# Gains applied while a normed activation is split in two, and a new order of the first loads, in a fp32 transformer kernel

## The chip, the cores and the metric

The kernel runs on one core of one Trainium2 chip. The metric is the time of one execution on the device in microseconds (us). The core has five engines with programs of their own that meet only in semaphores: TensorE (PE in the profile) multiplies matrices, VectorE (DVE) and ScalarE (ACT) work on 128 rows at a time, GpSimd (POOL) does so too, and SyncE (SP) issues loads. Loads are carried out by DMA queues; each engine that issues loads has a queue.

## The reference

The input x has 256 tokens of 1024 features, fp32. Two layers run over it, each of three residual steps: a gated feed-forward, a mixer (windowed attention and a short convolution), a gated feed-forward. A norm, a second block of one layer with two kinds of attention, and a last product follow.

```python
def rms_norm(x, gain):
    inv = lax.rsqrt(jnp.mean(x * x, axis=-1, keepdims=True) + NORM_EPS)
    return (x * inv) * gain
for l in range(DEPTH):
    x = x + 0.5 * swiglu(rms_norm(x, ffn1_norm[l]), wg, wu, wd)      # 1024 -> 2816 -> 1024
    z = rms_norm(x, mix_norm[l]) @ w_in[l]                           # attention, convolution
    x = x + mixed @ w_out[l]
    x = x + 0.5 * swiglu(rms_norm(x, ffn2_norm[l]), wg, wu, wd)
x = rms_norm(x, final_norm)
```

## The kernel before

Everything lies transposed: features on the 128 partitions, tokens in the columns. x is kept as eight tiles of 128 features by 256 tokens (`x_res`, KT = 8).

**Split products.** fp32 accuracy comes from three products of reduced-precision parts. A weight tile w (128 x 1024, 512 KB) is loaded into one of four slots of `w_raw`; ScalarE rounds it to `w_hi` (L408), VectorE takes the rest w - w_hi as `w_lo` (L676), and TensorE does hi x hi, lo x hi, hi x lo (L1064 to L1066), 24 products of 256 columns for an output tile of 128 features. SP loads the weights in the order of use; a load waits until the slot's `w_lo` is done. `split_ahead` splits three weight tiles ahead of the one in use.

**The norm.** The root mean square scales columns (tokens) and so may be applied after the product; the gain scales rows and goes in before. For each of the eight tiles k of x:
- ScalarE squares the tile (`square`, L420); GpSimd adds the squares of tiles 0 to 6 up in turn (L345, L348, `acc_step`); TensorE sums over the partitions with a matrix of ones (L1096, and L1098 for the square of tile 7).
- VectorE multiplies by the gain (`scaled`, L689) into a buffer `h_32`, ScalarE rounds that to `h_hi` (`high`, L438), VectorE subtracts to get `h_lo` (`low`, L695).

These stand in four places. At the start, for k = 0 to 7, with the splits of the first three weight tiles between them: the first behind tile 3. In `down` (the last product of each feed-forward), where every second weight tile completes one output tile of x. In `wout` (the mixer's last product), where each weight tile does. In both, VectorE first adds the product to x (L751, L861), then `scaled`, `low`. In `wout` it also splits a weight tile between the two. A norm of its own after the last layer (`norm`, L702, L433) uses `h_32` too and has its gain and root applied at once.

**TensorE behind a norm** (`first_pair`): bank 0 takes the tiles 0 to 6 as their `h_lo` come, then the two sums, then bank 1 takes the tiles 0 to 6, and both take tile 7. Behind the last layer there is no first pair; only the sums stand there, and Ln and Exp on ScalarE wait for them.

**The first loads.** SP issues x in two halves of 512 KB, then the weight tiles. ScalarE issues a small table with all gains. GpSimd issues the loads of constants (2.3 MB, used 200 us later) once the eighth `scaled` is done.

## Time and profile before

| | before |
|---|---|
| median of 3 runs | 1277.93 us (1277.87 to 1278.14) |
| the profiled execution | 1275.89 us, of which the span from the first to the last instruction is 1274.1 |
| TensorE's matmuls, busy | 1239.2 us, 97% of the span |
| VectorE, ScalarE, GpSimd busy | 822.2, 658.6, 147.2 us |
| weight split, ScalarE (L408) and VectorE (L676), mean | 1.1 and 1.3 us |
| small table (57 KB), issued by ScalarE | from 1.24, for 0.40 us |
| chain that ended last | 92% TensorE, 4% VectorE, 2% ScalarE |

The profiled execution is a little shorter than the median. Busy time says what an engine did, not that the others waited for it; what counts is idle time of TensorE and the engine that ends it. Matmuls overlap, so two of them are compared by their starts.

### The profile page before, as it was taken

The page shows a single profiled execution, that of the slowest core. Times are in us where ns is not written, and L with a number is a line of the kernel's source. Part 1 is how long each engine was busy: PE and PEld are TensorE (multiplying, and loading weights), DVE is VectorE, ACT ScalarE, POOL GpSimd, SP SyncE. Part 2 cuts the span into 40 slices and gives each one's busy share as a digit, 9 for nine tenths or more (in the row PEclk, how much of TensorE's full clock was granted, in tenths as well). Part 3 has the DMA queues.
Part 4 walks back from the last instruction along what each step waited for, and adds up shares of the span by engine and source line. Part 5 has one row for each costly group of instructions (what it writes and reads, how often), then busy time and mean ns, then how long its engine had stood idle before and what let it go on. Part 6 is the DMA issues. An engine that isn't in the chain of part 4 may idle for free.

```text
span 1274.1 us, 27430 instructions
## 1 busy us (share of the span) xinstructions
PE 1239.2 (97%) x10074; PEld 1191.6 (94%) x10074; DVE 822.2 (65%) x1378; ACT 658.6 (52%) x1105; POOL 147.2 (12%) x209
## 2 busy tenths in 40 slices
PE   6999999999999999999999999999989989999998
PEld 6999999999999999999999999999978878987888
DVE  6667665867666655667656777667657666535664
ACT  6445543646544545445544555545445656644652
POOL 3000000351000000000001340000021000002540
PEclk9999999999999999999999999999998999999999
DMA  7555654345556644555644346556633320435442
GB/s 285 185 190 186 236 168 144 133 133 199 181 181 207 220 167 151 181 187 202 222 148 165 117 149 198 181 181 224 204 120 121 124 100 22 161 100 174 149 141 83
DMA packets 56197, 210.89 MB, mean 166 GB/s; under 512 B 6672, under 2 KB 8720, under 8 KB 56000
## 3 DMA queue, kind: packets, MB, share of 16 engines
q1 hardware_dynamic: 54048, 203.45, 47.1%
q0 software_dynamic: 1936, 6.47, 1.6%
q8 instruction: 42, 0.69, 0.2%
q14 instruction: 27, 0.22, 0.1%
q10 hardware_dynamic: 144, 0.06, 0.0%
HBM read 208.91 MB, written 1.05 MB: 165 GB/s over the span
## 4 chain that ended last, share of the span: by engine, by line
PE 92%; DVE 4%; ACT 2%; issue 2%; DMA 0%; POOL 0%; DVEq 0%; ACTq 0%; SPq 0%; POOLq 0%
PE bank L1064 27%; PE bank L1066 26%; PE bank L1065 26%; PE bank L1389 2%; DVE w_lo L676 2%; PE bank L1102 1%; PE bank L1372 1%; DVE h_lo L695 1%; PE bank L1359 1%; PE bank L1300 1%; PE bank L1302 1%; PE bank L1301 1%; ACT w_hi L408 1%; PE bank L1354 1%; PE bank L1157 0%
## 5 line engine op out<-in xcount | busy, mean ns | idle before, releaser
L1064 PE MATMUL bank<-h_hi,w_hi 128*128 128x256 f32 (+1 forms) x1992 | 570.3, 286 | 17.3 <-DVE w_lo L676 11.7
L1065 PE MATMUL bank<-h_lo,w_hi 128*128 128x256 f32 (+1 forms) x1992 | 563.0, 283 | 0.0
L1066 PE MATMUL bank<-h_hi,w_lo 128*128 128x256 f32 (+1 forms) x1992 | 562.7, 282 | 0.0
L676 DVE TENSOR_TENSOR w_lo<-w_raw,w_hi 128x1024 fp32r<-128x1024 f32 (+1 forms) x360 | 465.9, 1296 | 81.2 <-ACT w_hi L408 80.5
L408 ACT ACTIVATE w_hi<-w_raw 128x1024 fp32r<-128x1024 f32 (+1 forms) x360 | 397.8, 1109 | 91.8 <-PE bank L1066 68.3
L1064 PEld LDWEIGHTS bank<-h_hi,w_hi 128*128 128x128 f32 x1992 | 378.2, 190 | 27.4 <-issue 22.9
L1066 PEld LDWEIGHTS bank<-h_hi,w_lo 128*128 128x128 f32 x1992 | 379.0, 190 | 0.0
L1065 PEld LDWEIGHTS bank<-h_lo,w_hi 128*128 128x128 f32 x1992 | 376.5, 189 | 0.9
L1064 PE MATMUL bank<-g_hi,w_hi 128*128 128x256 f32 x832 | 230.4, 277 | 0.8 <-DVE x_res L861 0.8
L1065 PE MATMUL bank<-g_lo,w_hi 128*128 128x256 f32 x832 | 229.8, 276 | 0.0
L1066 PE MATMUL bank<-g_hi,w_lo 128*128 128x256 f32 x832 | 229.8, 276 | 0.0
L1064 PEld LDWEIGHTS bank<-g_hi,w_hi 128*128 128x128 f32 x832 | 156.2, 188 | 1.6 <-issue 0.8
L1065 PEld LDWEIGHTS bank<-g_lo,w_hi 128*128 128x128 f32 x832 | 156.2, 188 | 0.0
L1066 PEld LDWEIGHTS bank<-g_hi,w_lo 128*128 128x128 f32 x832 | 156.2, 188 | 0.0
L460 ACT ACTIVATE g_hi<-gated 128x256 f32 (+1 forms) x88 | 37.0, 420 | 167.5 <-DVE gated L731 167.5
L727 DVE TENSOR_TENSOR gated<-bank,rstd 128x256 f32<-128x256 f32 x88 | 37.4, 424 | 97.7 <-PE bank L1066 97.4
L420 ACT ACTIVATE squares<-x_res 128x256 f32<-128x256 f32 (+2 forms) x64 | 26.7, 419 | 120.5 <-DVE x_res L751 97.3
L345 POOL COPY ln_mean<-squares 128x256 f32<-128x256 f32 (+1 forms) x8 | 5.3, 667 | 558.9 <-ACT squares L420 558.9
L456 ACT ACTIVATE silu_gate<-squares 128x256 f32<-128x256 f32 x88 | 37.0, 420 | 59.4 <-DVE squares L723 59.4
L723 DVE TENSOR_TENSOR squares<-bank,rstd 128x256 f32<-128x256 f32 x88 | 37.4, 424 | 46.7 <-PE bank L1066 46.7
L348 POOL TENSOR_TENSOR ln_mean<-ln_mean,squares 128x256 f32<-128x256 f32 (+1 forms) x45 | 44.3, 984 | 183.5 <-ACT squares L420 183.0
L1064 PE MATMUL bank<-y_hi,w_hi 128*128 128x256 f32 (+1 forms) x168 | 50.1, 298 | 0.0
(153 smaller groups left out, 1189.3 us busy)
## 6 DMA issues: line engine op xcount, KB each, us to landing
w_raw<-in_w SPq DMA_DIRECT2D x296, 512.0 KB, 3.3
w_raw<-in_wd SPq DMA_DIRECT2D x64, 704.0 KB, 4.1
rel_bias<-in_relbias POOLq DMA_DIRECT2D x32, 128.0 KB, 2.4
btab_sb<-in_btab POOLq DMA_DIRECT2D x1, 1536.0 KB, 9.6
x_res<-in_xT SPq DMA_DIRECT2D x2, 512.0 KB, 5.0
out_T<-x_res SPq DMA_DIRECT2D x8, 128.0 KB, 1.7
rope_sb<-in_rope POOLq DMA_DIRECT2D x1, 272.0 KB, 3.5
mats_sb<-in_mats POOLq DMA_DIRECT2D x1, 192.0 KB, 3.9
```

What stands on the lines that cost most here:

```text
L348: pool.tensor_tensor(acc[:, 0:n], acc[:, 0:n], sq[:, k % 2, 0:n], ALU.add)\
L408: act.activation(whi[:, slot, 0:cols], raw[:, slot, 0:cols], ACT.Copy).then_inc(hi_ready[slot], 1)
L420: act.activation(sq[:, p, 0:src.shape[-1]], src, ACT.Square).then_inc(sq_done[p], 1)
L456: act.activation(sg[:, p], sq[:, p, 0:T], ACT.Silu).then_inc(silu_done[p], 1)
L460: act.activation(ghi[:, f, :], g32[:, p], ACT.Copy).then_inc(g_hi[p], 1)
L676: dve.tensor_tensor(wlo[:, slot, 0:cols], raw[:, slot, 0:cols], whi[:, slot, 0:cols].bitcast(F32), ALU.subtract).then_inc(lo_ready[slot], 1)
L723: dve.tensor_tensor(sq[:, p, 0:T], bank[2 * p][:, 0:T], rs[:, 0, 0:T], ALU.mult)\
L727: dve.tensor_tensor(g32[:, p], bank[2 * p + 1][:, 0:T], rs[:, 0, 0:T], ALU.mult)\
L1064: pe.matmul(o, h, xh, start=first, stop=False)
L1065: pe.matmul(o, h, xl, start=False, stop=False)
L1066: return pe.matmul(o, lo, xh, start=False, stop=last)
L1389: mm = pe.matmul(o, w, PT[:, v % 4, n * BLK:(n + 1) * BLK], start=n == 0, stop=n == 2)
```

## The change

Four things change together.
- `scaled` goes; `h_32` stays for `norm` alone. `high` reads x itself with the gain as its per-partition scale (a pointer into the table); `low` is one instruction x * gain - h_hi with three operands. In `down` and `wout`, ScalarE does `high` ahead of `square`.
- At the start x comes in four quarters of 256 KB from ScalarE's queue, behind the small table. SP starts with the first weight tile, and waits for the second quarter of x before the second weight tile.
- At the start VectorE does the squares of the odd tiles. The first weight tile is split behind tile 1 (the other two behind tiles 5 and 7, as before on ScalarE).
- GpSimd's loads of constants wait for the eighth `h_lo`.

```diff
@@ -211,7 +211,7 @@
         hi_ready = [sem(f"hi_ready{s}") for s in range(SLOTS)]
         lo_ready = [sem(f"lo_ready{s}") for s in range(SLOTS)]
         w_used = [sem(f"w_used{s}") for s in range(SLOTS)]
-        x_loaded = [sem(f"x_loaded{p}") for p in range(2)]
+        x_loaded = [sem(f"x_loaded{p}") for p in range(KT // 2)]
         g_loaded = sem("g_loaded")
         c_loaded, b_loaded = sem("c_loaded"), sem("b_loaded")
         const_set, second_set = sem("const_set"), sem("second_set")
@@ -292,9 +292,6 @@
         def _(sp):
             for s in raw_full:
                 sp.sem_inc(s, 16 * PRIME)
-            for p in range(2):
-                half = slice(p * KT // 2, (p + 1) * KT // 2)
-                sp.dma_start(x[:, half, 0:T], xT[:, half]).then_inc(x_loaded[p], 16)
 
             def load(src, cols, slot, count):
 
@@ -311,6 +308,8 @@
 
                 with sp.Fori(0, ph.pieces // SLOTS) as j:
                     for r in range(SLOTS):
+                        if name == "gu1" and r == 1:
+                            sp.wait_ge(x_loaded[1], 16)
                         piece(r, j)
                 for i in range(ph.pieces // SLOTS * SLOTS, ph.pieces):
                     piece(i, 0)
@@ -349,7 +348,7 @@
                             .then_inc(acc_step, 1)
 
             add_squares(0)
-            pool.wait_ge(h32_done, KT)
+            pool.wait_ge(h_lo, KT)
             pool.dma_start(mat[:], mats).then_inc(c_loaded, 16)
             pool.dma_start(rop[:], rope).then_inc(c_loaded, 16)
             pool.dma_start(cmask[:], colmask).then_inc(c_loaded, 16)
@@ -401,6 +400,9 @@
             for s in (*hi_ready, *silu_done, pt_done):
                 act.sem_inc(s, PRIME)
             act.dma_start(sml[:], small).then_inc(g_loaded, 16)
+            for p in range(KT // 2):
+                two = slice(2 * p, 2 * p + 2)
+                act.dma_start(x[:, two, 0:T], xT[:, two]).then_inc(x_loaded[p], 16)
 
             def split(slot, cols, count):
                 act.wait_ge(raw_full[slot], count * 16)
@@ -429,13 +431,13 @@
                 act.wait_ge(sum_done, q + 1)
                 rstd(bank[SUM][:, 0:n], 0, D, n, q + 1)
                 for k in range(KT):
-                    act.wait_ge(h32_done, q * KT + k + 1)
+                    act.wait_ge(h32_done, k + 1)
                     act.activation(hhi[:, k * TM:k * TM + n], h32[:, k % 4, 0:n], ACT.Copy).then_inc(h_hi, 1)
 
-            def high(q, k, slot):
-
-                act.wait_ge(h32_done, q * KT + k + 1)
-                act.activation(hhi[:, bass.ds(k * TM, T)], h32[:, slot, 0:T], ACT.Copy).then_inc(h_hi, 1)
+            def high(q, k):
+
+                act.activation(hhi[:, bass.ds(k * TM, T)], x[:, k, 0:T], ACT.Copy,
+                               scale=sml[:, bass.ds(q * KT + k, 1)]).then_inc(h_hi, 1)
 
             def late_rstd(q):
                 act.wait_ge(sum_done, q + 1)
@@ -475,10 +477,10 @@
                         split_ahead(name, nxt, l, i, j, last)
                         if r % 2:
                             p, o2 = r // 2, j if not last else KT // 2 - 1
+                            act.wait_ge(x_ready[p], q * 4 + o2 + (PRIME - 3))
                             act.wait_ge(acc_step, q * 7 + o2 * 2 + p - 1)
-                            act.wait_ge(x_ready[p], q * 4 + o2 + (PRIME - 3))
+                            high(q, o2 * 2 + p)
                             square(p, x[:, o2 * 2 + p, 0:T])
-                            high(q, o2 * 2 + p, p)
 
                 with act.Fori(0, DN // SLOTS - 1) as j:
                     lap(j, False)
@@ -538,20 +540,22 @@
                         act.wait_ge(sum_done, q)
                     else:
                         act.wait_ge(acc_step, q * 7 + o - 1)
+                    high(q, o)
                     square(o % 2, x[:, o, 0:T])
-                    high(q, o, o % 2)
                     if o == KT - 1:
                         split_ahead("wout", "gu2", l, o)
 
             act.preload_act_table_set("natural_log_exp_and_others")
+            act.wait_ge(g_loaded, 16)
             for k in range(KT):
-                act.wait_ge(x_loaded[k // (KT // 2)], 16)
-                if k >= 2:
-                    act.wait_ge(acc_step, k - 1)
-                square(k % 2, x[:, k, 0:T])
-                high(0, k, k % 4)
-                if k in (3, 5, 7):
-                    split((k - 3) // 2, PT8, uses0(1))
+                act.wait_ge(x_loaded[k // 2], 16)
+                if k % 2 == 0:
+                    if k >= 2:
+                        act.wait_ge(acc_step, k - 1)
+                    square(0, x[:, k, 0:T])
+                high(0, k)
+                if k in (1, 5, 7):
+                    split((1, 5, 7).index(k), PT8, uses0(1))
             with act.Fori(0, LAYERS) as l:
                 late_rstd(l * 3)
                 gate_up("gu1", "dn1", l, 0)
@@ -684,16 +688,12 @@
                 else:
                     split(ph.slot(t), ph.cols, uses(name, t, l, j))
 
-            def scaled(q, k, slot):
-
-                dve.tensor_scalar(h32[:, slot, 0:T], x[:, k, 0:T], sml[:, bass.ds(q * KT + k, 1)], None, ALU.mult)\
-                   .then_inc(h32_done, 1)
-
-            def low(q, k, slot):
+            def low(q, k):
+
                 dve.wait_ge(h_hi, q * KT + k + 1)
                 h = bass.ds(k * TM, T)
-                dve.tensor_tensor(hlo[:, h], h32[:, slot, 0:T], hhi[:, h].bitcast(F32), ALU.subtract)\
-                   .then_inc(h_lo, 1)
+                dve.scalar_tensor_tensor(out=hlo[:, h], in0=x[:, k, 0:T], scalar=sml[:, bass.ds(q * KT + k, 1)],
+                                         in1=hhi[:, h].bitcast(F32), op0=ALU.mult, op1=ALU.subtract).then_inc(h_lo, 1)
 
             def norm(q, n=T):
                 dve.wait_ge(rstd_done, q + 1)
@@ -751,8 +751,7 @@
                             dve.scalar_tensor_tensor(out=xo, in0=bank[4 + p][:, 0:T], scalar=0.5, in1=xo,
                                                      op0=ALU.mult, op1=ALU.add).then_inc(x_ready[p], 1)
                             dve.wait_ge(x_ready[p], q * 4 + o2 + (PRIME - 3))
-                            scaled(q, o2 * 2 + p, p)
-                            low(q, o2 * 2 + p, p)
+                            low(q, o2 * 2 + p)
 
                 with dve.Fori(0, DN // SLOTS - 1) as j:
                     lap(j, False)
@@ -860,22 +859,22 @@
                     xo = x[:, o, 0:T]
                     dve.tensor_tensor(xo, bank[2 + o % 2][:, 0:T], xo, ALU.add).then_inc(x_ready[o % 2], 1)
                     dve.wait_ge(x_ready[o % 2], q * 4 + (o // 2 + PRIME - 3))
-                    scaled(q, o, o % 2)
                     if o < KT - 1:
                         split_ahead("wout", "gu2", l, o)
-                    low(q, o, o % 2)
+                    low(q, o)
                     if o == KT - 1:
                         split_ahead("wout", "gu2", l, o)
 
             dve.wait_ge(g_loaded, 16)
-            for k in range(KT + 1):
-                if k < KT:
-                    dve.wait_ge(x_loaded[k // (KT // 2)], 16)
-                    scaled(0, k, k % 4)
-                if k > 0:
-                    low(0, k - 1, (k - 1) % 4)
-                if k in (4, 6, 8):
-                    split((k - 4) // 2, PT8, uses0(1))
+            for k in range(KT):
+                dve.wait_ge(x_loaded[k // 2], 16)
+                if k % 2:
+                    if k >= 2:
+                        dve.wait_ge(acc_step, k - 1)
+                    dve.tensor_tensor(sq[:, 1, 0:T], x[:, k, 0:T], x[:, k, 0:T], ALU.mult).then_inc(sq_done[1], 1)
+                low(0, k)
+                if k in (1, 5, 7):
+                    split((1, 5, 7).index(k), PT8, uses0(1))
             with dve.Fori(0, LAYERS) as l:
                 gate_up("gu1", "dn1", l, 0, l * 3)
                 down("dn1", "qkv", l, l * 3 + 1)
```

## Rows read from the trace of the kernel before

**Rows 1.** TensorE's waits, whole run: who was waited for, us in total, times, longest.
```profile
PE bank L1064 <- DVE w_lo L676: 11.7, 1, 11.7
...
PE bank L1064 <- DVE h_lo L695: 2.3, 1, 2.3
```

**Rows 2.** Loads in short stretches of the start: count, KB each, us to landing.
```profile
x_res<-in_xT SPq DMA_DIRECT2D x1, 512.0 KB, 4.6
...
w_raw<-in_w SPq DMA_DIRECT2D x1, 512.0 KB, 5.6
...
w_raw<-in_w SPq DMA_DIRECT2D x1, 512.0 KB, 3.2
```

**Rows 3.** Timeline of VectorE, start: start, us, line, out<-in [idle before <-releaser].
```profile
5.66 0.62 DVE L689 TENSOR_SCALAR h<-x_res,small_sb 128x256 f32<-128x256 f32 x2 [5.66 <-DMA x_res<-in_xT]
...
13.62 1.23 DVE L676 TENSOR_TENSOR w_lo<-w_raw,w_hi 128x1024 fp32r<-128x1024 f32 x1
14.76 0.83 DVE L689 TENSOR_SCALAR h<-x_res,small_sb 128x256 f32<-128x256 f32 x1
15.52 0.41 DVE L695 TENSOR_TENSOR h_lo<-h,h_hi 128x256 fp32r<-128x256 f32 x1
```

**Rows 4.** Timeline of GpSimd, start.
```profile
13.97 1.48 POOL L348 TENSOR_TENSOR ln_mean<-ln_mean,squares 128x256 f32<-128x256 f32 x1 [0.86 <-ACT squares L420]
```

**Rows 5.** The accumulator's tile in the first 18 us: ns least, median, most.
```profile
L348 POOL TENSOR_TENSOR ln_mean<-ln_mean,squares x6: 724/930/1478, 6.9 to 14.0; 128x256 f32<-128x256 f32 x6
```

**Rows 6.** Timeline of TensorE, start: its first product, and tile 6 of bank 0.
```profile
11.72 0.58 PE L1064 MATMUL bank<-h_hi,w_hi 128*128 128x256 f32 x1 [11.72 <-DVE w_lo L676]
...
15.98 0.42 PE L1064 MATMUL bank<-h_hi,w_hi 128*128 128x256 f32 x1
```

**Rows 7.** Timeline of VectorE in `wout` of the first layer, one output tile.
```profile
279.97 0.41 DVE L861 TENSOR_TENSOR x_res<-bank,x_res 128x256 f32<-128x256 f32 x1
280.52 0.36 DVE L689 TENSOR_SCALAR h<-x_res,small_sb 128x256 f32<-128x256 f32 x1
280.79 1.22 DVE L676 TENSOR_TENSOR w_lo<-w_raw,w_hi 128x1024 fp32r<-128x1024 f32 x1
281.93 0.97 DVE L695 TENSOR_TENSOR h_lo<-h,h_hi 128x256 fp32r<-128x256 f32 x1
282.82 0.41 DVE L861 TENSOR_TENSOR x_res<-bank,x_res 128x256 f32<-128x256 f32 x1
```

**Rows 8.** Timeline of TensorE: 34 products of `down`, then holes in `wout`.
```profile
195.79 0.28 PE L1066 MATMUL bank<-g_hi,w_lo 128*128 128x256 f32 x1
...
199.53 0.28 PE L1066 MATMUL bank<-g_hi,w_lo 128*128 128x256 f32 x1
...
286.07 0.28 PE L1066 MATMUL bank<-g_hi,w_lo 128*128 128x256 f32 x1
286.58 0.36 PE L1064 MATMUL bank<-g_hi,w_hi 128*128 128x256 f32 x1 [0.23 <-DVE x_res L861]
...
294.23 0.28 PE L1066 MATMUL bank<-h_hi,w_lo 128*128 128x256 f32 x1
294.66 0.39 PE L1064 MATMUL bank<-h_hi,w_hi 128*128 128x256 f32 x1
```

**Rows 9.** Timeline of ScalarE at the end of the last `down`.
```profile
946.07 0.42 ACT L420 ACTIVATE squares<-x_res 128x256 f32<-128x256 f32 x1 [3.20 <-DVE x_res L751]
```

**Rows 10.** Timeline of TensorE at the same place.
```profile
946.54 0.70 PE L1098 MATMUL bank<-squares,ones_sb 128*128 128x256 f32 x2 [0.59 <-ACT squares L420]
```

**Rows 11.** Groups of instructions by shape: busy us, mean ns, idle before.
```profile
L966 DVE SCALAR_TENSOR_TENSOR q_heads<-bank,small_sb,rstd 128x256 f32<-128x256 f32 x16 | 7.8, 484 | 14.0 <-ACT rstd L425 14.0
...
L498 ACT ACTIVATE probs<-scores_sb,neg_max 128x256 f32<-128x256 f32 x16 | 7.9, 497 | 0.0
...
L751 DVE SCALAR_TENSOR_TENSOR x_res<-bank,x_res 128x256 f32 x24 | 10.2, 425 | 17.1 <-PE bank L1066 17.1
```

**Rows 12.** Stretches of the start: length, TensorE's busy us (starts), clock, DMA share, GB/s.
```profile
11.70:15.50 3.80, 3.78 (x17) 1.00 0.40 138
16.00:20.00 4.00, 4.00 (x30) 1.00 0.83 267
```

## The prediction, made before the changed kernel ran

> **What bounds the kernel now.** I read the page first: TensorE is busy for 97% of the span, so an edit counts only where TensorE waits for somebody. The next view is the table of TensorE's waits [rows 1]. It names 11.7 us at the start and one wait of 2.3 us on h_lo. The 2.3 us stand at the only turn of the outer loop, and TensorE then begins with feature tile 0, the first written of the eight. I take them for the jump, which the edit does not touch. So three places are left: the start, the two "wout" stages, and the last norm of the first block, where TensorE waits for a square.
>
> **The start before.** The first half of x is issued at 0.99 and lands 4.6 us later [rows 2]; VectorE begins at 5.66 [rows 3]. TensorE starts at 11.72, and the seventh tile of bank 0 starts at 15.98, directly behind h_lo at 15.52 + 0.41 = 15.93 [rows 3, 6]. From there on TensorE has no gap for a whole stage. What counts is therefore not when TensorE starts but when h_lo of tile 6 ends: 15.93 - 5.55 = 10.4 us behind the landing of x.
> What fills these 10.4 us is seen by laying GpSimd's row beside VectorE's. The add at 13.97 takes 1.48 us, though it has only 256 columns, and ends at 15.45: 0.6 us behind the end of w_lo at 14.85. The scaling at 14.76 takes 0.83 us and ends at 15.59, 0.14 behind the add [rows 3, 4]. The two engines take turns. An add holds VectorE up for about 0.65 us (15.45 - 14.85 = 0.60, and 0.72 in the shortest add of the start [rows 5]); I use 0.67. The Trainium skill (SBUF — State Buffer, section "SBUF: two separate sides") says that VectorE with two SBUF inputs, or in a two-port mode, and GpSimd lock each other out for a whole instruction. By that rule, the trace agrees.
> Sum for before: first tile 1.3 (scale 0.31, high 0.42, low 0.41, hand-overs), six further tiles of scale 0.15 + low 0.33 + add 0.67 = 1.15, so 6.9, and two w_lo at 1.15 each, 2.3: 10.5 against the measured 10.4.
>
> **The start after.** (a) The eight scalings go: their visible share was 0.15 each, since the adds covered the rest. (b) Low becomes a three-operand instruction with a pointer scalar. The nearest row of that shape takes 0.484 [rows 11] against 0.41 to 0.43 for low, so +0.06 each; lower bound 0. (c) High reads a pointer scale; no row has that, but Exp with a pointer bias and 256 columns takes 0.497 [rows 11] against the 0.42 of a square without one [rows 9]: +0.08; lower bound 0. It is on the path only in the first tile. (d) Three odd squares (1, 3, 5) move to VectorE ahead of low 6, 0.33 each. (e) The first weight tile is split after tile 1 instead of tile 3, the second still after tile 5. Both w_lo stay in front of low 6.
> The same sum: first tile 1.4, six tiles of 0.39 + 0.67 = 1.06, so 6.4, three squares 1.0, two w_lo 2.3: 11.1 us. Some of the adds may fall into time in which VectorE waits for the earlier w_hi anyway; one or two of 0.67 each could vanish so, which gives 9.8 as the other end. I take 10.4, the same as before: the middle of the two ends.
> When x lands: the first quarter goes as 256 KB on ScalarE's queue behind the small table while the first weight tile runs beside it. The table and a weight tile are now ahead of it or with it, 0.52 + 0.06 + 0.26 = 0.84 MB, where before 0.52 + 0.06 MB were. A lone weight load takes 3.2 us from issue to landing [rows 2]. The first quarter is issued at about 1.7 (the issue of the table takes ScalarE from 1.24 to 1.64): with the 3.2 of a lone load it lands at 4.9, with the 4.6 of the first half of x at 6.3. I take 5.6, unchanged; the ends are 0.7 either way. So low 6 ends at about 16.0. Start: 0 us, from -1.4 (loss) to +1.2 (gain).
> The second weight tile now waits for half of x (about 6.6) and is followed by two more on SP's queue; all weight loads stand behind that wait. At 3.2 us alone, or 5.0 with the x quarters ahead of it, it lands at 9.8 to 11.6 (the first tile of before, issued with 1.1 MB of x and table on the way, took 5.6 [rows 2]; that would be 12.2). It is split after tile 5, and w_lo 1 starts by my sum at about t = 14, so it has 0.7 to 3 us to spare beyond the 1.1 of its w_hi. GpSimd's loads of constants wait for h_lo 8 instead of the eighth scaling: 1 us later, and needed 200 us later. Cost 0.
> The tail of the norm (Ln, Exp, table load) hangs on the sums, behind low 6; nothing in it changes.
>
> **"wout", twice.** VectorE does per output tile: residual 0.41, scale 0.36, w_lo 1.22, low 0.97 (0.41 and a wait for the add), and its period is 282.82 - 279.97 = 2.85 us [rows 7]. TensorE needs 24 products; where it has no hole, 33 intervals take 199.53 - 195.79 = 3.74 us, 0.1133 each [rows 8], so 2.72 us a tile. So VectorE is the bound here, by 0.13 a tile. It shows as two holes of TensorE, 0.51 and 0.43 from start to start where 0.11 is normal, so 0.40 + 0.32; and the 65 intervals between them take 294.23 - 286.58 = 7.65 us, 0.118 each, which is 0.3 over the hole-less spacing, of which I count 0.2 [rows 8]. Without the scaling the next instruction starts 0.27 sooner (280.79 - 280.52); low costs 0.06 more: period 2.64, under 2.72. The order on ScalarE, high now ahead of the square, starts the add 0.5 later, yet still within w_lo, behind which it waited already; so that is free. Both holes close: 0.9 us each stage, 1.8 in all. Ends: 0 if the period stays at 2.85, and 2.0 if all of the 0.3 comes back too.
>
> **"down", four times.** TensorE runs through all its tiles, and VectorE stands idle on it for 17.1 us before 24 of the residual updates, 0.7 each [rows 11]. Scalings leave idle time only: 0. In three of the four, tile 7 has the other products of the next stage as cover: 2.5 us for bank 0, then the sums. In the fourth, the last norm of the first block, nothing follows. There the square is at 946.07, TensorE's sum waits 0.59 us for it [rows 9, 10], and everything behind waits for the norm. With high ahead of the square, it comes 0.43 to 0.50 later: -0.5 us. By the Trainium skill (ScalarE: Activation LUTs, section "What ACT_TABLE_LOAD costs") a pointer operand adds about 93 ns to an ACTIVATE; with that the term would be 0.52 in place of 0.50.
>
> **Sum.** 0 + 1.8 - 0.5 = 1.3 us faster. The profiled execution took 1275.9 us (span 1274.1 and 1.8 around it), 2.0 below the median of 1277.9; a difference carries over, so 1274.6 there and 1276.6 as the median.
>
> **Rivals.**
> A, the forecast: 0.60; from 1275.0 to 1278.4.
> B, the start gives its whole lead, because adds and VectorE's work overlap better than I think. The first w_hi starts at 5.6 + 1.1, takes 1.1, w_lo 1.2, hand-overs 0.3, and TensorE starts at 9.3 in place of 11.72; six tiles, 18 products at the slow spacing of 0.22 [rows 12], are 4.0 us, so the seventh tile of bank 0 starts at 13.3, 2.7 us sooner. 1277.9 - 2.7 - 1.8 + 0.5 = 1273.9. For it speaks that TensorE's start surely moves; against it, the taking of turns in [rows 3, 4]. 0.18.
> C, slower: TensorE's clock. Its first products are spaced 0.22 us (17 in 3.8), later ones 0.13 (30 in 4.0, the slower sums among them) [rows 12]; 1.2 and 2.4 GHz by the spacing, though the clock column says 1.00 in both, so the page does not record the change. Before the rise TensorE had worked without a hole to 15.5 (3.78 of 3.80 us). After, it starts at about 9.5 and has holes of 0.5 to 2 us before tiles 5 and 6. If the rise is put off past the sums, each product costs 0.10 more. Twenty of them cost 2.0 (time 1278.6); it becomes slower by the bound used here when 1.3 + 2.6 = 3.9 us are lost, 39 products. 0.12.
> D, "wout" gives nothing, since VectorE's period stays bound by the adds: 1277.9 + 0.5 = 1278.4. The measured low of 0.97 speaks for it, the 0.27 removed against it. 0.10.
> The chances: measurements here can tell about 0.2% (2.6 us). B is faster, with a little of A's edge: 0.20. A third of C and a bit of a late second weight tile are slower: 0.07. Same: 0.73. The range, 1274.2 to 1279.0, leaves out half of B and the far end of C.
>
> **What would show it.** In the changed profile: TensorE's first product at 9 to 10 us; the seventh tile of bank 0 still near 16; adds of GpSimd over 1 us beside w_lo; w_lo of the second tile ending before 15. In "wout": a period of VectorE of 2.72 with idle time in it, and no hole of TensorE but the first; low at about 0.48 alone. At the last norm: high, then square, and TensorE's wait 1.0 instead of 0.6. The prediction fails if h_lo of tile 6 ends at 13.5 (B), if product spacings of 0.22 are still there behind the sums (C), or if x's first quarter lands after 7.

## The result, and the profile after

The changed kernel takes 1278.84 us (median of 20 runs) against 1277.26 for the kernel before (20 runs): 1.6 us slower by the medians, ratio of the runs 1.0014, interval 1.0008 to 1.0020. The forecast was 1.3 us faster. The time lies within the range given, and on the other side of no change. Of all runs below one was slow as a whole, a run of e1 with 1531.28 us at a granted clock of 0.751, and it is left out. The profiled execution took 1278.54 us with a span of 1276.7, so 2.65 and 2.7 more than before's.

First the table of TensorE's waits, as in [rows 1]. The first wait is hardly shorter, h_lo is now waited for twice, and the last norm shows.

```profile
PE bank L1063 <- DVE w_lo L680: 11.4, 1, 11.4
...
PE bank L1063 <- DVE h_lo L695: 4.4, 2, 2.6
...
PE bank L1097 <- ACT squares L422: 1.1, 1, 1.1
```

The loads issued between 1.5 and 1.7 us (KB each, us from issue to landing), against [rows 2]. The first weight tile, issued at 1.57, lands in 3.4. The first quarter of x, half as large and issued at 1.64, needs 5.5.

```profile
w_raw<-in_w SPq DMA_DIRECT2D x1, 512.0 KB, 3.4
x_res<-in_xT ACTq DMA_DIRECT2D x1, 256.0 KB, 5.5
small_sb<-in_small ACTq DMA_DIRECT2D x1, 57.0 KB, 1.8
```

So the first square, whose wait ends with x, starts at 7.26. The timelines of ScalarE, VectorE, GpSimd and TensorE at the start, against [rows 3, 4, 6]:

```profile
7.26 0.42 ACT L422 ACTIVATE squares<-x_res 128x256 f32<-128x256 f32 x1 [2.29 <-DMA x_res<-in_xT]
```

```profile
13.49 0.95 DVE L874 TENSOR_TENSOR squares<-x_res 128x256 f32<-128x256 f32 x1
14.37 0.47 DVE L695 SCALAR_TENSOR_TENSOR h_lo<-x_res,small_sb,h_hi 128x256 fp32r<-128x256 f32 x1
14.76 1.75 DVE L680 TENSOR_TENSOR w_lo<-w_raw,w_hi 128x1024 fp32r<-128x1024 f32 x1
16.43 0.94 DVE L695 SCALAR_TENSOR_TENSOR h_lo<-x_res,small_sb,h_hi 128x256 fp32r<-128x256 f32 x1
```

```profile
14.52 2.57 POOL L347 TENSOR_TENSOR ln_mean<-ln_mean,squares 128x256 f32<-128x256 f32 x2 [0.36 <-DVE squares L874]
```

```profile
11.36 0.58 PE L1063 MATMUL bank<-h_hi,w_hi 128*128 128x256 f32 x1 [11.36 <-DVE w_lo L680]
...
15.32 0.28 PE L1065 MATMUL bank<-h_hi,w_lo 128*128 128x256 f32 x1
17.43 0.39 PE L1063 MATMUL bank<-h_hi,w_hi 128*128 128x256 f32 x1 [1.83 <-DVE h_lo L695]
...
17.89 0.59 PE L1095 MATMUL bank<-ln_mean,ones_sb 128*128 128x256 f32 x2
```

h_lo of tile 6 ends at 16.43 + 0.94 = 17.37, 10.2 us behind the landing of x at about 7.2. TensorE starts its seventh tile at 17.43; in [rows 6] that was 15.98. The sums stand at 17.89 (before: 16.48). The two adds, 2.57 together, lie beside a w_lo and a low. An instruction of VectorE that starts while an add runs is 0.4 to 0.5 longer than its like alone (w_lo 1.75 and, at 18.03, 1.21; low 0.94); the low at 14.37, which starts 0.15 ahead of the add, keeps its 0.47. The accumulator's tile in these us, against [rows 5], has the same six adds of about 0.9 us:

```profile
L347 POOL TENSOR_TENSOR ln_mean<-ln_mean,squares x6: 735/908/1522, 9.1 to 15.6; 128x256 f32<-128x256 f32 x6
```

The hole of 2.11 us has an echo in the clock. Stretches of the start, columns as in [rows 12] with the other engines between:

```profile
11.70:15.50 3.80, 3.80 (x18) 3.44 (x17) 3.80 (x7) 3.41 (x8) 2.55 (x3) 1.00 0.88 327
16.00:20.00 4.00, 2.57 (x12) 2.40 (x13) 3.24 (x5) 1.17 (x3) 2.68 (x4) 0.82 0.48 159
18.00:20.00 2.00, 2.00 (x10) 1.82 (x9) 1.24 (x2) 0.75 (x2) 1.59 (x3) 0.63 0.84 268
20.00:22.00 2.00, 2.00 (x12) 2.00 (x11) 0.00 (x0) 1.97 (x3) 2.00 (x4) 0.52 0.92 326
22.00:24.00 2.00, 2.00 (x19) 2.00 (x19) 0.56 (x2) 0.52 (x2) 0.14 (x1) 1.00 1.07 350
```

Behind the hole the granted clock is 0.52, and TensorE, busy all the time, starts 12 products in 2 us; in the next stretch, at 1.00, it starts 19. At the sums behind the first `down` the kernel is 2.98 us behind the kernel before (205.09 against 202.11), of which 1.41 were there at 17.9. The other 1.57 are the slow products.

In `wout`, against [rows 7, 8], VectorE's timeline has a period of 284.76 - 282.29 = 2.47 and the next of 2.57:

```profile
282.29 0.41 DVE L860 TENSOR_TENSOR x_res<-bank,x_res 128x256 f32<-128x256 f32 x1
282.73 1.23 DVE L680 TENSOR_TENSOR w_lo<-w_raw,w_hi 128x1024 fp32r<-128x1024 f32 x1
283.87 0.97 DVE L695 SCALAR_TENSOR_TENSOR h_lo<-x_res,small_sb,h_hi 128x256 fp32r<-128x256 f32 x1
284.76 0.41 DVE L860 TENSOR_TENSOR x_res<-bank,x_res 128x256 f32<-128x256 f32 x1
```

TensorE keeps only the first hole, at 277.60, 0.46 from start to start (before: 274.62, 0.45); the two of [rows 8] are gone. From the sums behind `down` to those behind `wout` it takes 296.95 - 205.09 = 91.86 us, before 93.01: 1.15 less, and 1.16 in the second layer.

The groups by shape, against [rows 11]: low with three operands and a pointer takes 713 ns on average where adds run beside it (the first group) and 485 in `down`, high 506 and 511.

```profile
L695 DVE SCALAR_TENSOR_TENSOR h_lo<-x_res,small_sb,h_hi 128x256 fp32r<-128x256 f32 x32 | 22.8, 713 | 16.9 <-ACT h_hi L439 16.9
L439 ACT ACTIVATE h_hi<-x_res,small_sb 128x256 fp32r<-128x256 f32 x32 | 15.8, 506 | 40.3 <-DVE x_res L751 26.5 <-DVE x_res L860 13.8
L439 ACT ACTIVATE h_hi<-x_res,small_sb x24 | 12.3, 511 | 77.2 <-DVE x_res L751 77.2
L695 DVE SCALAR_TENSOR_TENSOR h_lo<-x_res,small_sb,h_hi x24 | 11.6, 485 | 25.0 <-ACT h_hi L439 25.0
```

At the turn of the outer loop the hole is 482.87 - 480.00 = 2.87 from start to start (before: 2.55), and here too a slow clock follows, which the profiled execution of before did not have. TensorE's timeline and the stretches behind it:

```profile
480.00 0.28 PE L1065 MATMUL bank<-g_hi,w_lo 128*128 128x256 f32 x1
482.87 0.58 PE L1063 MATMUL bank<-h_hi,w_hi 128*128 128x256 f32 x1 [2.59 <-DVE h_lo L695]
483.24 0.42 PE L1064 MATMUL bank<-h_lo,w_hi 128*128 128x256 f32 x1
```

```profile
482.00:484.00 2.00, 1.13 (x5) 1.14 (x6) 0.08 (x1) 0.00 (x0) 0.00 (x0) 0.68 0.09 25
484.00:486.00 2.00, 2.00 (x11) 2.00 (x11) 0.00 (x0) 0.00 (x0) 0.00 (x0) 0.50 0.02 8
486.00:488.00 2.00, 2.00 (x15) 1.90 (x14) 0.00 (x0) 0.03 (x1) 0.00 (x0) 0.96 0.00 0
```

At the last norm, against [rows 9, 10], high goes first on ScalarE, and TensorE's sum waits 1.11 in place of 0.59:

```profile
948.46 0.51 ACT L439 ACTIVATE h_hi<-x_res,small_sb 128x256 fp32r<-128x256 f32 x1 [3.33 <-DVE x_res L751]
948.87 0.40 ACT L422 ACTIVATE squares<-x_res 128x256 f32<-128x256 f32 x1
```

```profile
949.33 0.70 PE L1097 MATMUL bank<-squares,ones_sb 128*128 128x256 f32 x2 [1.11 <-ACT squares L422]
```

The account of the two profiled executions, by TensorE's place at each milestone (behind the kernel before, us):

| milestone | before | after | behind | added by the part |
|---|---|---|---|---|
| sums of the start | 16.48 | 17.89 | 1.41 | 1.41 |
| sums behind the first `down` | 202.11 | 205.09 | 2.98 | 1.57 |
| sums behind the first `wout` | 295.12 | 296.95 | 1.83 | -1.15 |
| sums behind the turn | 483.40 | 486.91 | 3.51 | 1.68 |
| sums behind the next `down` | 669.04 | 672.57 | 3.53 | 0.02 |
| sums behind the second `wout` | 762.08 | 764.45 | 2.37 | -1.16 |
| second sum of the last norm | 946.54 | 949.33 | 2.79 | 0.42 |
| end | 1274.06 | 1276.74 | 2.68 | -0.11 |

### The profile page after: what moved, and what is told of

Read it like the earlier page. It is cut to its first block, busy times and chain, and to the rows that moved or that the text cites. A ratio compares the mean times of both kernels' runs of the same rounds, so it can differ in the third digit from the quotient of the medians.

```text
span 1276.7 us, 27358 instructions
## 1 busy us (share of the span) xinstructions
PE 1240.5 (97%) x10074; PEld 1193.7 (93%) x10074; DVE 806.2 (63%) x1326; ACT 655.9 (51%) x1101; POOL 140.5 (11%) x209
## 3 DMA queue, kind: packets, MB, share of 16 engines
q10 hardware_dynamic: 1232, 1.11, 0.3%
## 4 chain that ended last, share of the span: by engine, by line
PE 95%; ACT 2%; DVE 1%; issue 1%; DMA 0%; ACTq 0%; POOL 0%; DVEq 0%
PE bank L1063 28%; PE bank L1065 27%; PE bank L1064 27%; PE bank L1388 2%; PE bank L1101 2%; PE bank L1371 1%; PE bank L1358 1%; PE bank L1299 1%; PE bank L1301 1%; PE bank L1300 1%; PE bank L1353 1%; ACT w_hi L410 1%; PE bank L1156 0%; PE bank L1155 0%; DMA x_res<-in_xT 0%
## 5 line engine op out<-in xcount | busy, mean ns | idle before, releaser
L439 ACT ACTIVATE h_hi<-x_res,small_sb 128x256 fp32r<-128x256 f32 (+1 forms) x56 | 28.1, 508 | 117.4 <-DVE x_res L751 103.7
L695 DVE SCALAR_TENSOR_TENSOR h_lo<-x_res,small_sb,h_hi 128x256 fp32r<-128x256 f32 (+1 forms) x56 | 34.5, 615 | 41.9 <-ACT h_hi L439 41.9
L347 POOL TENSOR_TENSOR ln_mean<-ln_mean,squares 128x256 f32<-128x256 f32 (+1 forms) x45 | 39.0, 866 | 183.8 <-ACT squares L422 181.3
```

Source lines behind the costliest of these rows:

```text
L347: pool.tensor_tensor(acc[:, 0:n], acc[:, 0:n], sq[:, k % 2, 0:n], ALU.add)\
L439: act.activation(hhi[:, bass.ds(k * TM, T)], x[:, k, 0:T], ACT.Copy, scale=sml[:, bass.ds(q * KT + k, 1)]).then_inc(h_hi, 1)
L695: dve.scalar_tensor_tensor(out=hlo[:, h], in0=x[:, k, 0:T], scalar=sml[:, bass.ds(q * KT + k, 1)], in1=hhi[:, h].bitcast(F32), op0=ALU.mul ...
```

## The experiments

Twelve kernels ran. Ratios are to the kernel before in the same session, with 95% intervals. Its median was 1277.26 beside after (20 runs), 1276.41 beside e1 to e4 (35), 1277.19 beside e5 to e9 (27) and 1277.52 beside e10 to e13 (13), so kernels of different sessions are compared by ratios. All ratios lie within 0.6% of 1. "Low 6" is the end of h_lo of tile 6 behind the landing of x; landings and the two columns behind them are of one profiled execution each, and the last column says whether the granted clock fell behind the turn of the outer loop in the profiled execution.

| kernel | us | ratio (interval) | x lands | low 6 behind it | sums of the start | clock falls at turn |
|---|---|---|---|---|---|---|
| before | see above | 1 | 5.55 | 10.4 | 16.48 | no |
| after | 1278.84 | 1.0014 (1.0008 to 1.0020) | 7.2 | 10.2 | 17.89 | yes |
| e1 loads as before | 1277.37 | 1.0003 (0.9991 to 1.0015) | 5.55 | 11.25 | 17.66 | no |
| e2 direct parts alone | 1273.99 | 0.9981 (0.9972 to 0.9990) | 5.8 | 9.0 | 15.89 | yes |
| e3 new loads alone | 1277.79 | 1.0010 (1.0001 to 1.0019) | 7.4 | 10.4 | 18.67 | yes |
| e4 square first | 1275.83 | 0.9995 (0.9986 to 1.0004) | 7.6 | 10.2 | 18.63 | no |
| e5 before, turn written out | 1273.51 | 0.9971 (0.9959 to 0.9983) | 5.4 | 10.4 | 16.63 | no |
| e6 old order at the start | 1276.18 | 0.9996 (0.9987 to 1.0005) | 7.0 | 9.0 | 16.69 | yes |
| e8 narrow adds | 1274.37 | 0.9979 (0.9969 to 0.9989) | 7.2 | 7.4 | 15.49 | yes |
| e9 direct parts, quarters on SP | 1274.65 | 0.9980 (0.9970 to 0.9989) | 5.0 | 10.6 | 16.15 | yes |
| e10 direct parts, turn written out | 1270.74 | 0.9946 (0.9933 to 0.9960) | 5.8 | 9.0 | 15.36 | no |
| e11 after, turn written out | 1274.20 | 0.9976 (0.9965 to 0.9986) | 6.3 | 10.1 | 17.28 | no |
| e12 e10, odd squares on VectorE | 1271.97 | 0.9961 (0.9948 to 0.9975) | 5.8 | 10.1 | 16.42 | no |
| e13 e10, first split behind tile 1 | 1272.74 | 0.9963 (0.9949 to 0.9977) | 5.9 | 10.4 | 17.19 | no |

Three rows have the same code at the start: after, e4 and e11. Low 6 is 10.1 to 10.2 us behind the landing in all three, but the landing is at 7.2, 7.6 and 6.3, and the sums are at 17.89, 18.63 and 17.28. One profile therefore gives the time behind the landing well, and the landing itself only to about 1 us.

The first theory was that x lands later, and that this alone moved the start. The second, that the work put ahead of low of tile 6 (odd squares, the early split) ate what the removed scalings gave. A third, that the turn of the loop belongs to the account.

**e1, after with the loads of before.**

```diff
+            for p in range(2):
+                half = slice(p * KT // 2, (p + 1) * KT // 2)
+                sp.dma_start(x[:, half, 0:T], xT[:, half]).then_inc(x_loaded[p], 16)
...
-                        if name == "gu1" and r == 1:
-                            sp.wait_ge(x_loaded[1], 16)
...
-            for p in range(KT // 2):
-                two = slice(2 * p, 2 * p + 2)
-                act.dma_start(x[:, two, 0:T], xT[:, two]).then_inc(x_loaded[p], 16)
```

> The changed kernel with the loads as before: x in two halves from SP ahead of all weight tiles, nothing waits for x on SP; squares, splits and parts as in the changed kernel. Theory 1 (the start lost because x's first quarter lands at 7.2 us in place of 5.5): x lands at 5.5 again, h_lo of tile 6 ends 10.2 us behind it at 15.7, no hole of TensorE over 1 us before the sums and so no fall of its clock there; 1.7 us from the landing and 1.6 from the clock come back, 1275.5 to 1277 where the changed kernel has 1278.8. Theory 2 (the start lost through the longer low and the odd squares on VectorE): h_lo of tile 6 stays behind 17, and the time stays within 0.5 us of the changed kernel.

It is neither of the two alone: x is back at 5.55, yet low 6 ends at 16.80, and the sums come only 0.2 sooner than after. ScalarE's timeline shows what took the 1.7 us: the split behind tile 1 now stands before a weight tile that lands late, and everything of tiles 2 and on stands behind the split.

```profile
8.21 1.06 ACT L408 ACTIVATE w_hi<-w_raw 128x1024 fp32r<-128x1024 f32 x1 [1.42 <-DMA w_raw<-in_w]
```

**e2, the direct high and low alone** (on before: loads, splits and squares at the start as they were, squares first in `down` and `wout`), and **e3, the new loads alone** (on before, with `scaled`). Two places of e2's edit, against before; e3's edit is the loads of after, the opposite of e1's:

```diff
-                            scaled(q, o2 * 2 + p, p)
-                            low(q, o2 * 2 + p, p)
+                            low(q, o2 * 2 + p)
...
-                high(0, k, k % 4)
+                high(0, k)
```

> The kernel before with the direct parts alone: high and low read x and the gain, no scaling; all squares on ScalarE and ahead of high everywhere, loads and the order of the splits as before. Theory 1: both wout stages gain 1.1 to 1.2 us as in the changed kernel's trace, the last norm loses nothing, and the start gains 0 to 1 us (seven times 0.15): 1277.3 - 2.3 - 0.5 = 1274.5. Theory 2: the start loses, h_lo of tile 6 ends behind 16.5, 1275 to 1276.

> The kernel before with the new loads alone: x in quarters on ScalarE's queue beside the first weight tile, the second tile waiting for half of x; scalings, squares and splits as before. Theory 1: x lands 1.7 us later, h_lo of tile 6 ends at 17.5, and everything is 1.7 to 3.5 us later, the larger number with a fall of TensorE's clock: 1279 to 1281 against 1277.3. Theory 2: the loads are innocent, 1277 to 1277.6.

e2 is faster than both kernels: low of tile 6 ends 9.0 us behind the landing, where before had 10.4, and `wout` takes 91.89, 1.12 less than before. e3 is 1.3 us slower than before, between its two theories (the interval of its ratio starts at 1.0001): x lands at about 7.4, low 6 ends 10.4 behind it as in before, the sums come at 18.67, 2.2 late, and `wout` is unchanged at 93.03.

**e4, after with square ahead of high in `down` and `wout`.**

```diff
-                            high(q, o2 * 2 + p)
                             square(p, x[:, o2 * 2 + p, 0:T])
+                            high(q, o2 * 2 + p)
...
-                    high(q, o)
                     square(o % 2, x[:, o, 0:T])
+                    high(q, o)
```

> The changed kernel with the square ahead of high again in down and wout (not at the start). Theory 1: the last norm of the first block gets its 0.5 us back, TensorE's wait for the square there falls from 1.1 to 0.6, wout is untouched: 1278.3 in place of 1278.8. Rival: the order matters for the adds of wout, and its holes come back, each of 0.3 to 0.4 us: 1278.8 or more.

The wait at the last norm is back to 0.61, 0.50 less than after, in TensorE's timeline:

```profile
948.24 0.70 PE L1097 MATMUL bank<-squares,ones_sb 128*128 128x256 f32 x2 [0.61 <-ACT squares L422]
```

Its ratio is further below after's than the 0.5 us of that place can explain (0.9995 against 1.0014, from two sessions). The turn, with a low clock behind it in after's profile and none in e4's, is the one further difference that the two profiles show in e4's favour; its start was later (sums at 18.63). What the rest is stays open.

**e5, before with TensorE's layer loop written out.**

```diff
-            with pe.Fori(0, LAYERS) as l:
+            for l in range(LAYERS):
```

> The kernel before with TensorE's loop over the two layers written out as straight code, nothing else. Theory 1 (the hole of 2.5 us between the layers is the jump of the loop, and the clock falls behind it in some executions): the hole shrinks to below 0.5 us, since h_lo and weights are there, and no low clock stands at 480; 2.1 us from the hole and up to 1.6 from the clock, 1273 to 1275 against 1276.4. Rival (the hole is a wait for tile 7's square or h_lo, as the table of waits names it): it stays at 2.5 us and so does the time.

The hole is gone: TensorE's last product of one layer and the first of the next are 0.12 apart.

```profile
478.71 0.28 PE L1066 MATMUL bank<-g_hi,w_lo 128*128 128x256 f32 x1
478.83 0.28 PE L1064 MATMUL bank<-h_hi,w_hi 128*128 128x256 f32 x1
```

The time falls by 3.7 us, more than the 2.4 of the hole. The runs point to the reason: its six lie between 1272.86 and 1273.99, all with a mean granted clock of 0.995, where the 27 of before in that session spread from 1274.13 to 1278.93. Those 27 fall into two groups: 13 have a mean clock of 0.995 or 0.996 and take up to 1276.59, and 14 have 0.993 and take 1277.19 or more. The two other sessions divide in the same way: of the 75 runs in all, 36 have a mean clock of 0.993 or less, and they take some 1.8 us longer than the other 39, without overlap. With the hole goes, by this reading, the slow clock that followed it in part of the executions. A mean does not say where in the run the clock was low; but none of the five profiles with the turn written out has a low clock there.

**e6, after with the start's squares on ScalarE and the splits behind tiles 3, 5, 7; e8, after with GpSimd's six adds of the start over 8 of 256 columns.** e8 leaves the sum of squares of the first norm incomplete in the other 248 columns.

```diff
-                if k in (1, 5, 7):
-                    split((1, 5, 7).index(k), PT8, uses0(1))
+                if k in (3, 5, 7):
+                    split((3, 5, 7).index(k), PT8, uses0(1))
```

```diff
-                        pool.tensor_tensor(acc[:, 0:n], acc[:, 0:n], sq[:, k % 2, 0:n], ALU.add)\
+                        m = 8 if q == 0 else n
+                        pool.tensor_tensor(acc[:, 0:m], acc[:, 0:m], sq[:, k % 2, 0:m], ALU.add)\
```

> The changed kernel with its start in the old order: all squares on ScalarE, the first weight tile split behind tile 3; new loads kept. Theory 1 (the odd squares on VectorE cost their 0.33 each and more): x's first quarter lands at 7.2 as in the changed kernel, h_lo of tile 6 ends 9.0 us behind it as with the parts alone, at 16.2 in place of 17.4, so 1.2 us sooner, 1277.5. Rival (the early split and the squares on VectorE help, and only the landing hurts): h_lo of tile 6 ends at 17.4 or later, time as the changed kernel's.

> The changed kernel with GpSimd's six adds at the start over 8 columns in place of 256 (the sum of squares of the first norm is left wrong in 248 columns), same order and waits. Theory 1 (an add of GpSimd holds VectorE up for its whole length): low and w_lo of the start fall to their own lengths, 0.48 and 1.22, and h_lo of tile 6 ends 3 to 4 us sooner, at 13.5 to 14.5. Rival (they are limited by ScalarE or by the loads): less than 1 us sooner, since the w_hi and high are not there earlier.

e6 keeps high ahead of square in `down` and `wout`. It has x at 7.0 and low of tile 6 again 9.0 behind it. With e2 that makes 9.0 twice, at two landings: the direct parts in the order of before keep that distance, the new order adds 1.2. The late landing remains (sums 16.69 against 15.89).
e8 shows that it is the adds that make VectorE slow. Its timeline has w_lo at 1.23 and low at 0.48 in the place where after has 1.75 and 0.94:

```profile
13.00 1.23 DVE L681 TENSOR_TENSOR w_lo<-w_raw,w_hi 128x1024 fp32r<-128x1024 f32 x1
14.14 0.48 DVE L696 SCALAR_TENSOR_TENSOR h_lo<-x_res,small_sb,h_hi 128x256 fp32r<-128x256 f32 x1
```

Low of tile 6 ends at 14.62, 2.8 us sooner than after, with the same loads and order. GpSimd, for its part, takes 0.38 for an add of 8 columns that meets nobody and 0.94 for one that meets a w_lo. By the Trainium skill (SBUF — State Buffer, section "SBUF: two separate sides") GpSimd and a VectorE instruction with two SBUF inputs share a pair of ports, and whichever starts first has it for its whole instruction. The trace agrees: w_lo and low, with two inputs each, lose their 0.5 with the long adds.

**e9, e2 with x in four quarters on SyncE's queue.**

```diff
-            for p in range(2):
-                half = slice(p * KT // 2, (p + 1) * KT // 2)
-                sp.dma_start(x[:, half, 0:T], xT[:, half]).then_inc(x_loaded[p], 16)
+            for p in range(KT // 2):
+                two = slice(2 * p, 2 * p + 2)
+                sp.dma_start(x[:, two, 0:T], xT[:, two]).then_inc(x_loaded[p], 16)
```

> The parts alone, with x in four quarters on SP's queue ahead of the weight tiles (in place of two halves). Theory 1 (what lands first decides, and nothing may run beside x): the first quarter lands about 1 us sooner than the first half, at 4.6, but the small table is there only at 5.3, so VectorE's first low ends 0.2 to 0.5 us sooner and h_lo of tile 6 too, 1273.6 against 1274.0 with the halves. Rival: two more issues on SP at 0.5 us each delay the first weight tile to 9.2, its w_hi waits, and it is 0 to 0.5 us slower than the halves.

Quarters bring nothing: the first quarter lands at 5.0, and the first square starts at 5.17 (the wait ends with the small table) instead of 5.8. But the first weight tile, with four issues ahead of it in the queue, is ready only at 9.5, and the sums come 0.3 later than in e2.

**e10 to e13, with the turn written out.** e10 is e2 with e5's edit; e11 is after with it. e12 and e13 each add one part of the new start order to e10.

```diff
+                if k % 2:
+                    if k >= 2:
+                        dve.wait_ge(acc_step, k - 1)
+                    dve.tensor_tensor(sq[:, 1, 0:T], x[:, k, 0:T], x[:, k, 0:T], ALU.mult).then_inc(sq_done[1], 1)
                 low(0, k)
```

```diff
-                if k in (3, 5, 7):
-                    split((3, 5, 7).index(k), PT8, uses0(1))
+                if k in (1, 5, 7):
+                    split((1, 5, 7).index(k), PT8, uses0(1))
```

> The kernel before with the direct high and low (squares first, loads and splits as before) and TensorE's layer loop written out. If the direct parts are worth 2.6 us to 3.3 us as measured alone and the jump with the slow clock behind it 3.7, and the two don't overlap, it takes 1277.2 - 3.0 - 3.7 = 1270.5. If some of the gain of the direct parts was only the slow clock falling less often at the layer turn, 1272 or more.

> The whole change, with TensorE's layer loop written out. The loss of the whole change against the kernel before was made of a start 1.4 us later, slow clock behind it of 1.6, 2.3 gained in wout, 0.5 lost at the last norm, and some 1.8 more at the layer turn. If the last term is chance (a clock that falls in some executions, whatever the kernel), this runs at 1273.5 + 1.4 + 1.6 - 2.3 + 0.5 = 1274.7 or a little less. If the change itself makes the turn dearer in another way than the jump, it stays above 1275.5.

> As the run with direct parts and the turn written out, but VectorE does the squares of the odd tiles at the start; x still comes in halves on SyncE's queue and the splits stay behind tiles 3, 5, 7. If the odd squares on VectorE cost their own time ahead of low of tile 6, that low ends 1.0 us later than without them, at about 15.8; TensorE may then have a short hole before tile 6, and the sums come 0.3 to 1 later. If it is only the early split that costs, low of tile 6 ends as without the odd squares, at about 14.8.

> As the run with direct parts and the turn written out, but the first weight tile is split behind tile 1 in place of 3 on ScalarE and VectorE; squares stay on ScalarE, loads as before. The weight tile is ready only at about 8.2 then, so ScalarE stands some 1.4 us in front of its split with tiles 2 and on behind it. If this order costs, low of tile 6 ends at 15.6 to 16.0 in place of 14.8 and the first product does not come before 10.8. If the wait is hidden, low of tile 6 stays at 14.8.

e10 is the best version, 6.8 us under before with five runs (its interval is 5 to 8.6 us); e2 and e5 alone gave 2.4 and 3.7, so the two gains add up, as far as five runs tell. Its start is the cleanest of all, with low of tile 6 (the first of two) done before TensorE asks for it:

```profile
14.38 0.87 DVE L691 SCALAR_TENSOR_TENSOR h_lo<-x_res,small_sb,h_hi 128x256 fp32r<-128x256 f32 x2
```

```profile
14.67 0.28 PE L1057 MATMUL bank<-h_hi,w_lo 128*128 128x256 f32 x1
14.91 0.39 PE L1055 MATMUL bank<-h_hi,w_hi 128*128 128x256 f32 x1
```

e12 shows the price of the odd squares: low of tile 6 starts at 14.96 with the add beside it and ends at 15.91, 1.1 later than e10's, and the median is 1.2 us longer (five runs each, with intervals that overlap). e13 shows the price of the early split where the weight tile is not there yet: ScalarE waits 1.12 for it, TensorE has a hole of 1.41 behind tile 5, in this timeline, and its products are 0.21 apart in front of it and behind it, the spacing of the slow clock (the clock column reads 1.00 there, as in [rows 12]):

```profile
14.98 0.41 PE L1057 MATMUL bank<-h_hi,w_lo 128*128 128x256 f32 x1
16.39 0.58 PE L1055 MATMUL bank<-h_hi,w_hi 128*128 128x256 f32 x1 [0.99 <-DVE h_lo L691]
16.77 0.41 PE L1056 MATMUL bank<-h_lo,w_hi 128*128 128x256 f32 x1
```

The sums come 1.8 later than in e10, and with the slow products behind them it is 3.1 at the sums of the first `down`; the median is 2.0 longer (five runs each, with intervals that overlap).
e11 takes 1274.20, close to the time that the sum without a dearer turn gave (1274.7). It is 0.7 us over e5, with intervals that overlap.

## Why the prediction was wrong

**The landing of x: the step that failed.** The prediction took the first quarter of x at 5.6, "unchanged; the ends are 0.7 either way". In after's profile it landed at 7.2, past both ends; the prediction had named a landing after 7 as a sign that it fails. The bounds came from two loads of 512 KB, a weight tile on its own (3.2) and the first half of x, issued ahead of everything else (4.6) [rows 2]; a quarter on a second queue beside a weight tile was taken for one of these. It took 5.5 us from issue for 256 KB while the weight tile, issued 0.07 earlier, took 3.4. The six profiles with the new loads have 4.6 to 5.9 for it, those with x in halves ahead of the weights 4.4 to 4.8 for the first half; the 4.6 is e11's, whose landing at 6.3 is the later end of the range given, and its sums still came 0.65 behind e5's. e3 shows the new loads alone: 1.3 us slower than before. Why the weight tile lands first is not settled. Its queue and the size of its packets differ from x's (to 14 us, ScalarE's queue moves 1.11 MB in 1232 packets, SyncE's 1.96 MB in 533), and no run separated the two.

**The time behind the landing: right as a middle, wrong in its parts.** The sum gave 11.1 us and the prediction took 10.4; after has 10.2. Without scalings and with the old order it is 9.0 (e2, e6, e10), where the same sum gives 10.1 (1.4, 6.4, 2.3): not all of the adds are visible, as the prediction allowed for. The odd squares cost 1.1 (summed: 1.0). The early split was put down at nothing, since "both w_lo stay in front of low 6". With the weight tile there in time, as after, that holds, for 9.0 and 1.1 make 10.1. With the loads of before it costs 1.4 (e13), through ScalarE's wait for the tile. So the two halves of the new start need each other, and each has a price: the order wants the weight tile first, and with the weight tile first x came late. Undone alone, neither brings e2's 0.9981 back: e1 (loads undone) has 1.0003 and e6 (order undone) 0.9996, after 1.0014.

**The clock: rival C, on top of the late start.** C was held for 12 in 100, as a rise put off by holes. What happened was near it: the rise came ahead of the hole (the products at 15.21 and 15.32 are 0.11 apart), the hole of 2.11 us followed, and behind it the granted clock is 0.52, the lower level of 1.2 GHz, for 1.57 us of loss. C's price was 2.0. In e4 and e11, with the same start, it was C as written: the products are 0.21 apart both before and behind a hole of 1.94, in e11's timeline:

```profile
14.54 0.41 PE L1065 MATMUL bank<-h_hi,w_lo 128*128 128x256 f32 x1
16.48 0.58 PE L1063 MATMUL bank<-h_hi,w_hi 128*128 128x256 f32 x1 [1.52 <-DVE h_lo L695]
16.86 0.41 PE L1064 MATMUL bank<-h_lo,w_hi 128*128 128x256 f32 x1
```

The large loss came with the hole. From the sums of the start to the next milestone the five profiles with a hole of 1.4 to 2.1 (after, e1, e4, e11, e13) take 186.8 to 187.2 us. Those without one over 0.7 take 185.6 to 186.2; before has 185.63, and e2 (186.16) lost 0.5 by a late rise alone. The prediction kept C apart from A as if the two were exclusive.

**"wout": right, and more.** 1.15 and 1.16 came back where 0.9 each was summed; with the 0.3 of tighter spacing, the far end of the range was 1.0 each. VectorE's period is 2.47 and 2.57 in turn, where 2.64 was summed, though low still takes 0.97 beside the add. That is under TensorE's 2.72 a tile, so TensorE has no hole. The sign named, 2.72 with idle time in it, did not come: VectorE has no idle time until the last tile. Since e2 has 1.12 with the square first, the gain is that of the scaling alone. D is out.

**"down": right.** 185.66 us from the sums behind the turn to those behind the next `down`, before 185.64.

**The last norm: right.** Forecast 0.5 us lost; the step between the two sums is 1.71 in place of 1.19, and e4 takes it back. A pointer operand costs ScalarE 0.09 (high 0.49 to 0.51, square 0.40 to 0.42). By the Trainium skill (ScalarE: Activation LUTs, section "What ACT_TABLE_LOAD costs") it is about 93 ns; the trace agrees.

**The turn of the loop: read rightly and left out wrongly.** The hole is the jump, as the prediction said, and e5 shows it. But it is no constant: the hole was 2.55 in one profile and 2.87 in the other, 2.47 to 3.47 in the nine with the loop, and behind it the clock falls in some executions. The length of the hole alone does not decide it: e4 had 3.07 and no fall, e6 2.51 and a fall. In the account above the turn is 1.68 of the 2.68 us. How much of it belongs to the change stays open. Only 3 of after's 20 runs have a mean granted clock of 0.995, against 39 of the 75 of before at 0.995 or more; but after has the slow stretch at its start as well, and the mean does not part the two. By medians the change costs 1.6 us with the loop and 0.7 without (e11 against e5), a difference that the intervals do not hold apart.

**Summed up.** Forecast, in us: start 0, wout -1.8, norm +0.5. Found: start +1.4, slow clock behind it +1.6, wout -2.3, norm +0.5: that is +1.2, and the turn makes up the rest of the 2.7 between the two profiles (the medians are 1.6 apart). That the time still lies in the range is partly luck: a start put at 0 cost 3.0, and `wout` paid for more of it than was forecast. The sign hung on the landing time and on the hole in front of tile 6, with the slow clock behind it.

## What to carry to other kernels

When loads are put on another queue, their landing is a number to be measured first, before the order of the work behind them is changed: here 256 KB beside a weight tile needed longer (4.6 to 5.9 us in six profiles) than 512 KB issued ahead of all weight tiles (4.4 to 4.8), and the chain of work behind the landing stayed as long as before (10.2 against 10.4). Take an edit apart: the gain applied while the parts are written was worth 2.4 us (e2), and what was changed beside it took 4.2 (ratio 1.0014 against 0.9981). And where an edit opens a hole of TensorE (1.4 to 2.1 us at the start here), count the slow products behind the hole as well as the hole; the profile of one execution may not have them.

## What the hardware did that was not expected

- The turn of TensorE's outer loop costs 2.4 us of idle time (2.55 in before against 0.12 in e5), and writing two turns out saves 3.7 in the median (ratio 0.9971, 0.9959 to 0.9983). The granted clock was low behind it in six of the nine kernels of this study that have the loop (before among the nine), and in none of the five without.
- With the turn written out, `wout` gains less from the change: 93.07 to 92.61 and 92.65 (e5, e11, e10), against 93.01 to 91.86 and 91.89 in the loop (before, after, e2). The loop is not what decides it, though: e1 has the loop and takes 92.49. Over the 165 products between the stage's first hole and the sums the spacing is 0.118 in e11, e10 and e1 and 0.114 or 0.115 in after and e2, without a further hole in any. What makes it is open, and nothing here was tried on it. It is 0.7 us a layer that e10 leaves.
- Order of landing does not follow order of issue across queues. With the new loads the weight tile, issued at 1.57, landed at 5.0 to 5.7, ahead of the first quarter of x (6.3 to 7.6) in every profile. The small table of 57 KB, issued at about 1.2, landed in 1.8 us with them, and in 4.1 with the old loads, where x was issued ahead of it on another queue.
